# The modulation vectors of a two-block transformer kernel: sums over partitions on VectorE and TensorE replaced by dot products along the free axis on VectorE

## The reference

```python
c_act = jax.nn.silu(c)
mod = (c_act @ w_mod[l] + b_mod[l]).reshape(c.shape[0], N_MOD, D_MODEL)
h = modulate(x, g_norm[l, 0], mod[:, 0], mod[:, 1])
x = x + 0.5 * mod[:, 2][:, None, :] * swiglu(h, w_ffn1_gu[l], w_ffn1_down[l])
...
mod = jax.nn.silu(c) @ w_ada[layer] + b_ada[layer]      # second block
mod_c = jax.nn.silu(c_ctx) @ w_ada[layer] + b_ada[layer]
```

## Time and profile before

| | |
|---|---|
| median of three executions | 2960.03 us (2958.96 to 2960.54) |
| the profiled execution, its own time | 2960.58 us |
| its span, first to last instruction | 2958.8 us |
| TensorE busy | 2814.6 us, 13036 matmuls |
| VectorE, ScalarE, GpSimd busy | 1459.2, 1012.2, 1136.2 us |
| mean granted TensorE clock | 0.972 of full speed |
| DMA | 374 MB, 127 GB/s on average |

### The profile page before, as it was taken

The page is one execution under the profiler, slowest core; times in us unless marked ns, Lnnn a source line. Parts: engine busy times, 40 slices in busy tenths (PEclk is TensorE's granted clock), DMA queues, the critical chain, the costliest instruction groups (busy, mean ns, idle before and its releaser), DMA issues.

```text
span 2958.8 us, 37062 instructions
## 1 busy us (share of the span) xinstructions
PE 2814.6 (95%) x13036; PEld 2288.0 (77%) x13036; DVE 1459.2 (49%) x2627; ACT 1012.2 (34%) x1449; POOL 1136.2 (38%) x488
## 2 busy tenths in 40 slices
PE   7999999999999999999989999988889999999997
PEld 4888877778888788887768888877666778788886
DVE  3525365554435543445745253654654555473645
ACT  2222235432222322224533222344444553243322
POOL 2444443234444444444233444453310323344433
PEclk9999999999999999999999999988999999999998
DMA  6535342135344354443214353632200114322221
GB/s 242 200 141 183 130 171 86 58 117 183 135 163 171 144 185 155 170 144 141 72 72 149 136 180 143 230 132 86 93 29 15 66 53 148 112 96 90 99 100 43
DMA packets 69269, 374.37 MB, mean 127 GB/s; under 512 B 7776, under 2 KB 8544, under 8 KB 38656
## 3 DMA queue, kind: packets, MB, share of 16 engines
q1 hardware_dynamic: 65424, 359.61, 33.9%
q10 hardware_dynamic: 3696, 12.85, 1.1%
HBM read 364.04 MB, written 8.39 MB: 126 GB/s over the span
## 4 chain that ended last, share of the span: by engine, by line
PE 37%; issue 32%; POOL 20%; DVE 4%; ACT 2%; DMA 1%; ACTq 1%; DVEq 1%; SPq 1%; POOLq 0%
POOL w_lo L407 20%; PE psum L472 9%; PE psum L473 9%; PE psum L474 9%; PE psum L878 2%; PE psum L900 1%; PE psum L491 1%; PE psum L493 1%; PE psum L492 1%; PE psum L888 1%; DVE psum L1918 1%; ACT w_hi L992 0%; PE psum L528 0%; SPq L368 0%; DMA raw<-in_weights_dram 0%
## 5 line engine op out<-in xcount | busy, mean ns | idle before, releaser
L407 POOL TENSOR_TENSOR w_lo<-raw,w_hi 128x1024 fp32r<-128x1024 f32 x464 | 1115.1, 2409 | 1664.3 <-ACT w_hi L992 1664.2
L472 PE MATMUL psum<-h_hi,w_hi 128*128 128x512 f32 x2080 | 820.6, 395 | 17.3 <-DVE h_lo L1437 16.6
L473 PE MATMUL psum<-h_lo,w_hi 128*128 128x512 f32 x2080 | 816.4, 392 | 0.0
L474 PE MATMUL psum<-h_hi,w_lo 128*128 128x512 f32 x2080 | 815.6, 392 | 0.0
L992 ACT CAST w_hi<-raw 128x1024 fp32r<-128x1024 f32 x464 | 482.5, 1049 | 886.7 <-PE psum L474 726.3
L472 PEld LDWEIGHTS psum<-h_hi,w_hi 128*128 128x128 f32 x2080 | 395.3, 190 | 104.6 <-DVE h_lo L1437 15.8
L473 PEld LDWEIGHTS psum<-h_lo,w_hi 128*128 128x128 f32 x2080 | 395.4, 190 | 82.4 <-issue 0.5
L474 PEld LDWEIGHTS psum<-h_hi,w_lo 128*128 128x128 f32 x2080 | 394.8, 190 | 83.0
L472 PE MATMUL psum<-hid_hi,w_hi 128*128 128x512 f32 x880 | 343.4, 390 | 5.5 <-DVE hid_lo L1924 5.5
L473 PE MATMUL psum<-hid_lo,w_hi 128*128 128x512 f32 x880 | 343.1, 390 | 0.0
L474 PE MATMUL psum<-hid_hi,w_lo 128*128 128x512 f32 x880 | 342.9, 390 | 0.0
(11 more groups left out here) (348 smaller groups left out, 3135.6 us busy)
## 6 DMA issues: line engine op xcount, KB each, us to landing
raw<-in_weights_dram SPq DMA_DIRECT2D x232, 1024.0 KB, 5.6
mod_raw<-in_mod_w_dram SPq DMA_DIRECT2D x192, 512.0 KB, 4.0
first_mods_a<-in_mod_w_dram SPq DMA_DIRECT2D x8, 512.0 KB, 11.9
first_mods_b<-in_mod_w_dram SPq DMA_DIRECT2D x8, 512.0 KB, 15.4
first_mods_a<-gate_spill ACTq DMA_DIRECT2D x4, 1024.0 KB, 12.1
gate_spill<-gate_out_c ACTq DMA_DIRECT2D x5, 512.0 KB, 3.0
x<-in_xT_dram SPq DMA_DIRECT2D x1, 2048.0 KB, 8.6
x_spill<-x ACTq DMA_DIRECT2D x1, 2048.0 KB, 12.6
```

What stands on the lines that cost most here:

```text
L407: pool.tensor_tensor(w_lo[:, k % 2, cs], raw[:, k % 4, cs], w_hi[:, k % 2, cs].bitcast(F32), ALU.subtract).then_inc(lo_ready, 1)
L472: pe.matmul(out, wh, rhs_hi[:, c, :], start=(c == ks[0]), stop=False)
L473: pe.matmul(out, wh, rhs_lo[:, c, :], start=False, stop=False)
L474: mm = pe.matmul(out, wl, rhs_hi[:, c, :], start=False, stop=(c == ks[-1]))
```

## The change

The weights of the 48 positions are laid out transposed: the output on the partitions, the 1024 inputs along the free axis, and piece p holds outputs 128 p to 128 p + 127. The condition row, the same on all partitions, is loaded by a DMA on ScalarE's queue into the tile `prod` (512 KB) and written through Silu into PSUM banks 6 and 7 by two activations (`row_fill`); it stays there for the feed-forward part or until the condition changes (eight times in all: positions 4, 16, 18, 22, 24, 28, 40, 42). VectorE forms each piece as one product with accumulated sum over 1024 columns (tensor_tensor_reduce), which gives 128 results in one column of `cond_now`; after four pieces the bias is added. macc, the copy of condition values, mod_split, mod_sum and, for these positions, mod_take go. On VectorE and ScalarE the loop over layers and the loop over thirds are unrolled; the other engines keep theirs.

```diff
+POS_COND = (0,) * 18 + (2,) * 4 + (1,) * 2 + (0,) * 18 + (1,) * 10
+STAGE_MODS = 12
+ROW_STARTS = tuple(p for p in range(FIRST_MODS, len(POS_COND))
+                   if (p - FIRST_MODS) % STAGE_MODS == 0 or POS_COND[p] != POS_COND[p - 1])
+def rows_until(pos):
+    return sum(p <= pos for p in ROW_STARTS)
...
-            def mod_sum(pos):
-                pe.wait_ge(macc_ready, pos - FIRST_MODS + 1)
-                pe.matmul(psum[:, O_BANK, :], ones_r[:, :], mod_parts[:, 0, :], start=True, stop=False)
-                pe.matmul(psum[:, O_BANK, :], ones_r[:, :], mod_parts[:, 1, :], start=False, stop=True).then_inc(msum_ready, 1)
...
-                        if pos is not None and j in (2, 4, 6, 8):
-                            mod_sum(pos + j // 2 - 1)
...
+            def row_load(pos):
+                act.dma_start(cond_row, a["cond_rows"][POS_COND[pos]]).then_inc(row_landed, 16)
+            def row_fill(pos):
+                act.wait_ge(row_landed, 16 * rows_until(pos))
+                act.wait_ge(mod_used, MOD_PIECES * (pos - FIRST_MODS) + 2)
+                for half in range(2):
+                    act.activation(psum[:, T_BANK + half, :], prod[:, half, :], ACT.Silu)
+                act.drain().then_inc(row_ready, 1)
+                r = rows_until(pos)
+                if r < len(ROW_STARTS) and (ROW_STARTS[r] - FIRST_MODS) % STAGE_MODS:
+                    row_load(ROW_STARTS[r])
...
+                        mod = pos + j // 2
+                        if j < 8 and j % 2 == 0 and mod in ROW_STARTS and (mod - FIRST_MODS) % STAGE_MODS:
+                            row_fill(mod)
...
+                act.wait_ge(t_ready, 8 * n + 1)
+                row_load(pos)
                 norm(n)
-                with act.Fori(0, 2) as i:
-                    third(g + 3 * i, k0, FC * f + 8 * i, 8, False)
-                third(g, k0 + 24, FC * f + 16, 6, True)
+                act.wait_ge(h_ready, 8 * n + 8)
+                row_fill(pos)
+                for i in range(2):
+                    third(g + 3 * i, k0, FC * f + 8 * i, pos + 4 * i, 8, False)
+                third(g, k0 + 24, FC * f + 16, pos + 8, 6, True)
...
             def mod_piece(pos, piece):
                 if piece == 0:
-                    dve.tensor_copy(cond_ps, cond[:, bass.ds(8 * pos, 8)])
-                dve.drain()
+                    dve.wait_ge(row_ready, rows_until(pos))
                 dve.wait_ge(mod_landed[piece % 2], 32 * (pos - FIRST_MODS) + 16 * (piece // 2 + 1))
-                for u in range(MOD_K):
-                    k = MOD_K * piece + u
-                    w = mod_raw[:, piece % 2, u, :]
-                    if k == 0:
-                        o = dve.tensor_scalar(macc, w, cond_ps[:, 0:1], None, ALU.mult)
-                    else:
-                        o = dve.scalar_tensor_tensor(macc, w, cond_ps[:, k:k + 1], macc, ALU.mult, ALU.add)
-                    if u < MOD_K - 1:
-                        dve.drain()
-                o.then_inc(mod_used, 1)
+                dve.tensor_tensor_reduce(mod_sink[:, :], mod_raw[:, piece % 2, :, :].rearrange("p k n -> p (k n)"), row_ps,
+                                         1.0, 0.0, ALU.mult, ALU.add, cond_now[:, piece:piece + 1])
+                dve.drain().then_inc(mod_used, 1)
+                if piece == MOD_PIECES - 1:
+                    dve.tensor_tensor(mods[:, 4 * pos:4 * pos + 4], cond_now[:, 0:4], mod_b[:, 4 * pos:4 * pos + 4], ALU.add)
+                    dve.drain()
...
-                        if j in (2, 4, 6, 8):
-                            mod_take(mod - 1)
                         if j < 8 and j % 2:
                             mod_piece(mod, 3)
-                            mod_split()
...
-            with dve.Fori(0, DEPTH) as l:
+            for l in range(DEPTH):
```

More of the change, by code:

```diff
@@ L122, in program @@
         turned_b, = region([("turned_b", [P, 2 * MOD_COLS], F32)])
-        mod_parts = sb("mod_parts", [P, 2, MOD_COLS], F32R)
+        mod_sink = sb("mod_sink", [P, MOD_K * MOD_COLS])
         ones_r = sb("ones_r", [P, P], F32R)
@@ L192, in program @@
         krope = mod_acc
+        cond_row = prod[:, :, :].rearrange("p a b -> p (a b)")
         w_decay = gates_all
@@ L211, in program @@
         mod_used = sem("mod_used")
-        macc_ready = sem("macc_ready")
+        row_landed = sem("row_landed")
+        row_ready = sem("row_ready")
         half_done = sem("half_done")
@@ L316, in program @@
         mod_cols = psum[:, T_BANK, 0:4]
-        cond_ps = psum[:, S_BANK + 1, 0:8]
+        row_ps = psum[:, T_BANK:T_BANK + 2, :].rearrange("p a b -> p (a b)")
         ssq_ps = psum[:, S_BANK, :]
@@ L1004, in norm, with ffn, third @@
                                    ).then_inc(h_hi_ready, 1)
-            def ffn(g, k0, n, f):
-                def third(g, k0, h0, count, last):
+            def row_load(pos):
[9 more added lines that the diff above has]
+                    row_load(ROW_STARTS[r])
+            def ffn(g, k0, n, f, pos):
+                def third(g, k0, h0, pos, count, last):
                     for j in range(count + 4):
@@ L1355, in _ @@
                 split_hi(0, k)
-            with act.Fori(0, DEPTH) as l:
+            for l in range(DEPTH):
                 g = l * (LAYER_BLOCKS // 4)
-                ffn(g, 0, 3 * l, 2 * l)
+                ffn(g, 0, 3 * l, 2 * l, LAYER_MODS * l + FIRST_MODS)
                 mixer(l, g, FFN_BLOCKS, 3 * l + 1)
-                ffn(g, FFN_BLOCKS + MIX_BLOCKS, 3 * l + 2, 2 * l + 1)
+                ffn(g, FFN_BLOCKS + MIX_BLOCKS, 3 * l + 2, 2 * l + 1, LAYER_MODS * l + FIRST_MODS + STAGE_MODS)
             second()
@@ L1499, in third @@
                             mod_piece(mod, 1)
-                with dve.Fori(0, 2) as i:
+                for i in range(2):
                     third(g + 3 * i, k0, FC * f + 8 * i, pos + 4 * i, 8, False)
@@ L2112, in layout @@
         cond = i["c"] if first else (i["c_2"] if l == 1 else i["c_ctx_2"])
-        ws.append(w[:, c * MOD_COLS:(c + 1) * MOD_COLS].reshape(MOD_PIECES, MOD_K, P, MOD_COLS).transpose(0, 2, 1, 3)
-                  .reshape(MOD_PIECES, P, MOD_K * MOD_COLS))
+        w = w[:, c * MOD_COLS:(c + 1) * MOD_COLS]
+        if len(ws) < FIRST_MODS:
+            w = w.reshape(MOD_PIECES, MOD_K, P, MOD_COLS).transpose(0, 2, 1, 3)
+        else:
+            w = w.T
+        ws.append(w.reshape(MOD_PIECES, P, MOD_K * MOD_COLS))
         bs.append(columns(np, b[c * MOD_COLS:(c + 1) * MOD_COLS]))
@@ L2119, in layout @@
     a["cond"] = np.concatenate(cs, 1)
+    a["cond_rows"] = np.stack([np.broadcast_to(np.asarray(i[name]).reshape(1, D), (P, D)) for name in ("c", "c_2", "c_ctx_2")])
     a["gains"] = np.concatenate([columns(np, i["g_norm"][l, s]) for l in range(DEPTH) for s in range(3)]
```

6 lines of the change are left out of this document (removed).

## The result

| | before | changed |
|---|---|---|
| median of the executions | 2960.28 us (2958.96 to 2962.6) | 2931.59 us (2930.03 to 2932.54) |
| ratio, 95% interval | | 0.9902 (0.989 to 0.9915) |
| profiled execution, its own time | 2960.58 us | 2931.22 us |
| its span | 2958.8 us | 2929.4 us |
| mean granted TensorE clock | 0.972 | 0.972 |

The account below looks back on a forecast made before the run. TensorE's own rate was taken to bound the feed-forward stretches, with the norm chain counting between them. −23.6 + 0 + 2.4 − 0.7 = −21.9 us gave 2938 us from a median near 2960; range 2933 to 2945, held at 0.81.

Parts of the forecast that it names:

- Sums on TensorE, −23.6: Feed-forward stretches: 48 modulation blocks each lose two TensorE matmuls, 44 x 0.453 + 4 x 0.91 us, all on the path.
- bare slots: Sums in the steady place of the stretches: TensorE loses two matmul slots and no more, 0.453 us each, 44 times.
- the four late ones: Sums in the last third of a stage, where VectorE is late with mod_parts: 0.91 us each.
- VectorE, nothing: VectorE's work per modulation block: four reductions of 1.4 us, 5.6 us, covered by TensorE's 21.8 us, so no effect.
- DMA issue on ScalarE, +2.4: Start of each feed-forward part: a DMA issue before the first h_hi, on the path, 4 x 0.6 us.
- the first rival: Row fill waits for the row's DMA and delays weight block 2 if landing over 19.5 us after issue; chance 0.04.
- the split of weight block 2: ScalarE's work behind the row fill at the start of a feed-forward part: ends some 2 us later, covered by TensorE.
- Unrolled loops, −0.7: VectorE and ScalarE loops: −0.5 us from var at the layer turn, −0.2 from register work ahead of the first norm.
- The second block, implicitly 0: Second block of the reference, code untouched: the prediction gave it no term, so no change.
- more than forecast: Rival: the DMA issue hides and the mixers give 2.5 us or more, below 2933 us; chance 0.03.
- waits for straight-line code: Rival: unrolled engines wait for instructions in the norms, up to 20 us lost; chance 0.08 for some, 0.02 for nearly all.

Follow-up runs that it names:

- e2: Kernel before without TensorE's 96 matmuls of the sums, so modulation values are not computed; loops kept: 2936.06 us, ratio 0.9912.
- e6: Changed kernel with two 128x512 matmuls, read by nobody, put back on TensorE where each sum stood: 2958.79 us, ratio 0.9993 to the kernel before.
- e1: Kernel before with only VectorE's and ScalarE's loops over layers and thirds unrolled: 2960.58 us, ratio 0.9999.
- e5: Kernel before without TensorE's 96 sum matmuls (values not computed) and with VectorE's and ScalarE's loops unrolled: 2932.79 us, ratio 0.9909.
- e8: Kernel before with two extra VectorE instructions, read by nobody, ahead of the first norm as a delay: 2963.91 us, ratio 1.0013.
- e9: Kernel before with four extra VectorE instructions, read by nobody, ahead of the first norm as a delay: 2967.01 us, ratio 1.0018.
- e7: Changed kernel again, unedited, on another chip: 2930.5 us, ratio 0.9897 to the kernel before.
- e3: Changed kernel with the row's DMA issue moved from ahead of the first h_hi to behind the last: 2932.37 us, ratio 0.9907 to the kernel before.

## Why the forecast was off

**Sums on TensorE, −23.6: right.** 23.3 us by the stretches of the changed kernel, 23.2 by those of e2, 22.3 given back in e6, where none is late. The bare slots show at 0.453 us as forecast (21.7 of the 22.3). The surplus of the four late ones was put at 1.8 us; as the difference between 23.3 and 22.3 it is 1.0, which is no more than the stretches differ by from kernel to kernel for other reasons (0.9 us in e1), so it is not shown apart. The lower price of the Trainium skill (TensorE: Matmul & The Clock Gate, section "Wait — 56ns, not 53.3ns?": 215.7 ns a matmul, 20.7 us for the 96 instead of 21.8) is not what this kernel shows: e6 has three matmuls in 0.68 us, 0.227 each.

**VectorE, nothing: right.** 1.30 us a dot product against 1.4; the stretches as full as before.

**DMA issue on ScalarE, +2.4: right in place, too large.** 0.334 to 0.398 us on ScalarE's queue and 0.38 to 0.45 us on the path, so +1.6. I had taken the issues that move gates to and from DRAM as nearest (0.52 to 0.73); this one is cheaper. The 50 ns of the Trainium skill (DMA: Bandwidth & Descriptors, section "Anatomy of one DMA — SWDGE (gpsimd) path"), told there for GpSimd's path, is about a seventh of it. The row landed in 3.4 to 3.6 us, so the first rival never came near its 19.5 us, and the split of weight block 2 started 12.0 us behind the first product of the norm (607.19 to 619.18) instead of 10.35, some 2 us later as forecast; TensorE waited 0.4 us in all for any w_lo.

**Unrolled loops, −0.7: the step that failed.** The prediction said: "TensorE keeps its own loop, so the rest of that pause stays." It did not stay. At the turn −2.6 us were measured where +0.1 was forecast. var at once behind TensorE gave its 0.6 about as worked out. The other two parts had been put at nothing: TensorE came back from its own jump 0.7 us sooner, and its sums ran at the upper clock, 1.6 us. Neither is the work of the unrolling alone. The return moved between two executions of the one changed kernel from 2.20 to 1.67 us, and over the kernels with TensorE's loop in place from 1.27 to 3.09; what sets it was not tried apart. The faster sums go with the products' absence: they are there in e2, with all loops in place, and not in e1, with the loops unrolled. They reach the path only where VectorE no longer comes last (e2 and e5). So the two halves of the change do not simply add at the turn, and the sum had priced each by itself. By the turns of e2 and e5 (12.03 and 10.08) and of before and e1 (12.84 and 11.31), none of which has a DMA issue there, the unrolling is worth 1.5 to 2 us; e8 and e9 reach 11.5 with all loops in place, so up to 1.3 us of that may be position alone.

**The second block, implicitly 0: −2.6, not forecast.** The code is the same. Aligning the two traces by instruction shows two places that make up most of it. One is the clock in the stage at 2010 us; windows over the same seven microseconds of work, before and then changed:

```profile
2007.50:2014.50 7.00, 7.00 (x17) 5.06 (x17) 0.59 (x2) 5.27 (x7) 1.77 (x1) 0.51 0.44 152
```

```profile
1980.50:1987.50 7.00, 6.55 (x21) 5.07 (x22) 0.85 (x3) 5.30 (x8) 2.37 (x1) 0.76 0.42 150
```

17 matmuls against 21 in 7 us; TensorE is 1.6 us further ahead behind them. The other is a wait that the changed kernel has not, in the timeline of the kernel before:

```profile
2508.85 0.39 PE L974 MATMUL psum<-yg_hi,w_lo 128*128 128x512 f32 x1
2510.37 0.47 PE L972 MATMUL psum<-om_hi,w_hi 128*128 128x512 f32 x1 [1.13 <-DVEq L1891]
```

1.52 − 0.227 = 1.3 us. Its cause was not tested, but the wait stands in the traces of all five kernels with the products or matmuls in their slots and in none of the seven without. The whole second block, whose code all share, took 1038.0 to 1040.7 us in those five and 1034.7 to 1037.8 in the seven. So this surplus, too, goes with the products' absence.

**The range** was built from this kernel's own terms alone, each at its end, and its lower end was 5 us below the forecast. It held nothing for the time of untouched code. The runs show 2 to 3 us either way between kernels: e7 repeats the changed kernel's span to 0.3 us, but an edit that moves the pauses gets other ones. Of the rivals, "more than forecast" came true by another way than the issue and the mixers, which it named. Of waits for straight-line code nothing was seen in the norms: at the turn VectorE's 4.57 us of idle marked issue went, and nothing like it came in its place.

On the clock itself: 512 columns at the lower level start 0.43 us apart here (608.21 to 608.64 in the changed kernel). The Trainium skill (TensorE: Matmul & The Clock Gate, section "Wait — 56ns, not 53.3ns?") gives 426.7 ns for this; the trace agrees. At the upper level they are 0.227 us apart here; the same section gives 215.7 ns, and the measurement decides.

## What to carry to other kernels

Price a step on the engine that is full by starts in the timeline, and count late steps apart from bare ones: the term of 23.6 us came out within 2%. In the pauses of that engine, read the granted clock too: an edit can change the level at which the work in a pause runs (1.6 us at the turn here), and whether that counts depends on which engine comes last there (in e2 VectorE's return hid it). Two edits that meet in one pause are therefore not priced one by one. Where an edit moves pauses, give the range 2 to 3 us either way for code that isn't touched, and before unrolling one engine's loop look at who else turns in the same pause: with ScalarE's and VectorE's loops unrolled alone the total did not move, with TensorE's as well (and the issue moved) the kernel gained another 4.6 us, of which only 0.3 show at the turn itself against e3.

## What the runs showed that was not expected

- The same instructions took 7.81, 8.72 or 9.10 us in one norm, at mean granted clocks of 0.86, 0.70 and 0.63, when the program in front was 2 to 3 us longer or not. Eight 128x1 column sums took 0.94 to 1.05 us at the upper level and 1.83 to 1.86 at the lower.
- A dot product over 1024 fp32 columns, one operand in SBUF and one in PSUM, took 1.22 us, and 0.08 us for the read of its accumulator.
- Behind the two Silus that fill the banks, ScalarE's drain took up to 1.63 us; here nobody waits for it but VectorE, 1.4 us in sum.
- With VectorE's loop over the layers unrolled and TensorE's sums (e1) or slots of the same size (e6) in place, the second mixer had one more wait of about 3 us for VectorE's register work; the traces of the other kernels do not show it. What brings it on is open.
